# Experts read the raw rows in steps of four columns, and one more expert weight unit is loaded ahead

## What is computed

```python
logits = einsum('bsd,de->bse', h, w_router)      # h = rmsnorm_2(x, norm_moe), 16 experts
aff = softmax(logits)
vals, idx = top_k(aff.T, cap)                    # cap = 32 tokens for each expert
xg = h[bidx, idx]                                # the gathered rows, 32 x 1024 per expert
h1, h3 = xg @ w1, xg @ w3                        # 1024 x 1024 each, per expert
out = (silu(h1) * h3) @ w2                       # 1024 x 1024
x = x + scatter_add(out * vals)
```

## Time and profile before

| | |
|---|---|
| median of three runs | 1896.9 us |
| the profiled execution, its own time | 1900.6 us |
| span from first to last instruction | 1898.8 us |
| PE busy, PE weight loads busy | 1550.6 us, 1135.1 us |
| DVE, ACT, POOL busy | 612.3, 500.4, 193.9 us |
| mean granted TensorE clock | 0.942 |
| moved by DMA | 563.65 MB, mean 297 GB/s |

### The profile page before, as it was taken

The page is one execution under the profiler, slowest core; times in us unless marked ns, Lnnn a source line. Parts: engine busy times, 40 slices in busy tenths (PEclk is TensorE's granted clock), DMA queues, the critical chain, the costliest instruction groups (busy, mean ns, idle before and its releaser), DMA issues.

```text
span 1898.8 us, 29516 instructions
## 1 busy us (share of the span) xinstructions
PE 1550.6 (82%) x12506; PEld 1135.1 (60%) x12506; DVE 612.3 (32%) x923; ACT 500.4 (26%) x910; POOL 193.9 (10%) x214
## 2 busy tenths in 40 slices
PE   7999999999999999665655656999998666666656
PEld 6999899998898886232322323997883322323225
DVE  3456534577556353000000002655450000000005
ACT  3433333556444432000000002454330000000003
POOL 0043000011041100000000002410100000000003
PEclk9999999999999999898888888999999888989888
DMA  8564549432554569999999999545399999999994
GB/s 284 164 219 168 195 155 301 152 111 91 178 172 136 177 233 386 425 427 424 427 426 424 427 426 377 180 152 178 128 378 394 426 425 424 427 425 427 426 425 152
DMA packets 166894, 563.65 MB, mean 297 GB/s; under 512 B 10559, under 2 KB 120027, under 8 KB 133896
## 3 DMA queue, kind: packets, MB, share of 16 engines
q1 hardware_dynamic: 159012, 552.08, 75.1%
q10 hardware_dynamic: 7780, 10.10, 1.6%
HBM read 561.08 MB, written 5.23 MB: 298 GB/s over the span
## 4 chain that ended last, share of the span: by engine, by line
PE 52%; DMA 36%; DVE 4%; ACT 3%; issue 3%; POOL 1%; SPq 0%; ACTq 0%; DVEq 0%; POOLq 0%
DMA ring<-in_moe_w 36%; PE bank L965 21%; PE bank L1213 7%; PE bank L1622 5%; PE bank L921 4%; PE bank L1060 3%; PE bank L1645 2%; PE bank L1276 2%; ACT ring_r L1695 1%; ACT big L1743 1%; PE bank L1090 1%; PE bank L1480 1%; PE bank L1285 1%; PE bank L1037 1%; PE bank L1651 1%
## 5 line engine op out<-in xcount | busy, mean ns | idle before, releaser
L1622 PE MATMUL bank<-ring,big 128*32 128x256 f32 x3840 | 281.3, 443 | 195.7 <-DMA ring<-in_moe_w 193.2
L1622 PEld LDWEIGHTS bank<-ring,big 128*32 128x32 f32 x3840 | 147.0, 123 | 335.8 <-issue 295.4
L965 PE MATMUL bank<-big_r,ring_r 128*128 128x256 f32 (+1 forms) x2760 | 344.1, 285 | 0.0
L965 PEld LDWEIGHTS bank<-big_r,ring_r 128*128 128x128 f32 (+1 forms) x2760 | 335.1, 191 | 3.0 <-issue 2.2
L2092 DVE TENSOR_TENSOR ring_r<-ring,ring_r 128x2048 fp32r<-128x2048 f32 (+2 forms) x105 | 243.0, 2319 | 135.3 <-ACT ring_r L1695 133.9
L1743 ACT ACTIVATE big<-bank 128x512 f32<-128x512 f32 (+2 forms) x186 | 87.9, 491 | 571.6 <-PE bank L921 366.8
L1695 ACT ACTIVATE ring_r<-ring 128x2048 fp32r<-128x2048 f32 (+2 forms) x109 | 204.2, 1881 | 10.4 <-DMA ring<-in_ev_w_out 5.1
L1645 PE MATMUL bank<-ring,big 128*32 128x512 f32 x1024 | 136.7, 634 | 74.0 <-DMA ring<-in_moe_w 55.5
L2479 DVE SCALAR_TENSOR_TENSOR big<-big,bank 128x256 f32<-128x256 f32 x32 | 13.5, 421 | 463.9 <-ACT big L1995 463.9
L1213 PE MATMUL bank<-ring_r,big_r 128*128 128x512 f32 x576 | 135.7, 395 | 0.7 <-DVE big_r L2099 0.7
L921 PE MATMUL bank<-big 128*128 128x128 f32 (+6 forms) x636 | 105.1, 292 | 35.7 <-ACT big L1743 18.2
(11 more groups left out here) (204 smaller groups left out, 1512.8 us busy)
## 6 DMA issues: line engine op xcount, KB each, us to landing
ring<-in_moe_w SPq DMA_DIRECT2D x120, 2048.0 KB, 23.7
ring<-in_moe_w SPq DMA_DIRECT2D x128, 1024.0 KB, 24.9
ring<-in_w_in SPq DMA_DIRECT2D x28, 1024.0 KB, 5.4
ring<-in_od_w_in SPq DMA_DIRECT2D x22, 1024.0 KB, 6.5
ring<-in_ev_w_in SPq DMA_DIRECT2D x20, 1024.0 KB, 7.3
big<-in_moe_w SPq DMA_DIRECT2D x8, 2048.0 KB, 11.2
ring<-in_ev_w_out SPq DMA_DIRECT2D x8, 1024.0 KB, 5.0
ring<-in_od_cmp_w SPq DMA_DIRECT2D x8, 1024.0 KB, 8.1
```

What stands on the lines that cost most here:

```text
L965: ins = unit[0].mark(mm(dst, lhsT, rhs, start=start and n == 0, stop=stop and n == len(terms) - 1))
L1622: ins = mm(banks[5 + up][32 * j:32 * j + 32, 0:256], xg[:, k, q, :], wv[:, r, 256 * j:256 * (j + 1)], start=k == 0, stop=k == KC - 1)
```

## The change

- The gather reads x itself as PE's stationary operand. The old copy put columns r, r+4, r+8, ... side by side; now the operand is a view of x with a step of four columns (16 bytes). `rows_u` and the `u_ready` wait are gone.
- The root goes into the one-hot matrix: DVE writes `onehot` in two halves of 128 columns, and after each half multiplies it by `rstd` into the new `rows_hot`, which is the gather's moving operand. `onehot` itself is kept for POOL. `rows_hot` lies where the `pw` product's input was, so DVE first waits for the last `pw` product.
- The gather's 16 products run by half of the columns, then by half of the rows, then four column blocks.
- `tile_ss` writes its unread squares to `pwb`, so `u` is free from the end of the attention. Into it SP loads expert 1's first down unit (`row_spare`, 1 MB), right after spares 1 and 2. Expert 1's other three down units go into the ring, and its fourth slot is passed over: PE marks it itself after the expert's down products.

```diff
-        spare_at = [G_at + 8 * T + 4 * D * i for i in range(SPARES - 1)] + [uT_at]
+        rows_hot = view(G_at + 8 * T + 4 * D * (SPARES - 1), P, TT, BATCH * CAP)
+        spare_at = [G_at + 8 * T + 4 * D * i for i in range(SPARES - 1)] + [uT_at, u_at]
...
+                def row_spare(row):
+                    src = flat(a["moe_w2_2"])[row:row + 2 * P, :].rearrange("(p r) c -> p (r c)", r=2)
+                    sp.dma_start(view(u_at, P, 2 * D), src).then_inc(spare_in[ROW_SPARE], 16)
+
-                def down(row):
-                    for i in range(4):
+                def down(row, first=0):
+                    for i in range(first, 4):
                         deep(a["moe_w2_2"], row + 256 * i, 2)
...
                 spare(1)
                 spare(2)
+                row_spare(first + D)
                 deep(ups[0], first, 4)
...
                 deep(ups[1], first + D, 4)
-                down(first + D)
+                down(first + D, 1)
+                w.next()
...
                 def batch(b):
                     g4 = l * (NE // BATCH) + b
-                    pe.wait_ge(onehot_ready, g4 + 1)
-                    for t in range(TT):
-                        pe.wait_ge(u_ready[t], rows_at(l, 1) + 1)
-                    for k in range(KC):
+                    for half in range(2):
                         for t in range(TT):
-                            ins = mm(banks[4 + 2 * (k // 4)][:, (k % 4) * P:(k % 4 + 1) * P], u[:, t, k * P:(k + 1) * P],
-                                     onehot[:, t].rearrange("p q s -> p (q s)"), start=t == 0, stop=t == TT - 1)
-                        if k % 4 == 3:
-                            ins.then_inc(gathered, 1)
+                            pe.wait_ge(onehot_ready, TT * g4 + t + 1)
+                            rows = x[:, t, 512 * half:512 * (half + 1)].rearrange("p (q r) -> p r q", r=4)
+                            for k in range(4):
+                                ins = mm(banks[4 + 2 * half][:, k * P:(k + 1) * P], rows[:, k, :], rows_hot[:, t, :],
+                                         start=t == 0 and k == 0, stop=t == TT - 1, skip_group_check=True)
+                        ins.then_inc(gathered, 1)
...
-                            U = Unit()
+                            U = Spare(l, ROW_SPARE) if isinstance(b, int) and (q, j) == (1, 0) else Unit()
...
+                        if isinstance(b, int) and q == 1:
+                            pe.sem_inc(units_in[w.next()[0]], 16)
+                            Unit.before += 1
...
-                tile_ss(0, x[:, 0, :])
+                tile_ss(0, x[:, 0, :], rest=pwb)
                 tile_raw(l, 0, gl[:, 8:])
-                rows_u(0)
...
+                wait_done(dve, l, "pw", 3)
                 stand(dve)
...
-                    V.tensor_tensor(onehot, con("iota").unsqueeze(1).unsqueeze(1).broadcast_to([P, TT, BATCH, CAP]),
-                                    idxT[:, :, bass.ds(b * BATCH, BATCH)].unsqueeze(3)
-                                    .broadcast_to([P, TT, BATCH, CAP]), ALU.is_equal).then_inc(onehot_ready, 1)
+                    for t in range(TT):
+                        steps.link(V.tensor_tensor(onehot[:, t], con("iota").unsqueeze(1).broadcast_to([P, BATCH, CAP]),
+                                                   idxT[:, t, bass.ds(b * BATCH, BATCH)].unsqueeze(2)
+                                                   .broadcast_to([P, BATCH, CAP]), ALU.is_equal))
+                        V.tensor_scalar(rows_hot[:, t, :], onehot[:, t].rearrange("p q s -> p (q s)"), rstd[:, t:t + 1], None,
+                                        ALU.mult).then_inc(onehot_ready, 1)
```

More of the change, by code:

```diff
@@ L290 @@
 SPARES = 4
+ROW_SPARE = SPARES
 PLE_AT, PER_LAYER = slots_of(PLE_UNITS, _n + NE * MOE_UNITS - 2 * SPARES)
@@ L567, in build @@
         uTh_ready = sem("uT_high")
-        spare_in = [sem(f"spare_in{i}") for i in range(SPARES)]
+        spare_in = [sem(f"spare_in{i}") for i in range(SPARES + 1)]
         units_in = [sem(f"unit_in{s}") for s in range(RING)]
@@ L688, in rows_at @@
         def rows_at(l, j):
-            return j if l is None else 3 + j + 2 * l
+            assert l is None or j == 0
+            return j if l is None else 3 + l
         def out_at(l, j):
@@ L910, in __init__ @@
                     pe.wait_ge(spare_in[i], 16 * (l + 1))
-                    s.words, s.first, s.step = view(spare_at[i], P, 4, D), True, Unit.before
+                    s.words = view(spare_at[i], P, 2 if i == ROW_SPARE else 4, D)
+                    s.first, s.step = True, Unit.before
                     Unit.before = 0
@@ L1678, in _, with tile_ss @@
             act.dma_start(perow, a["od_cmp_pe"][0].rearrange("v l d -> (v l) d")).then_inc(rows_in, 16)
-            def tile_ss(t, src, sums=ss):
-                A(u[:, t, :], src, ACT.Square, accum_out=sums[:, t:t + 1]).then_inc(norm_ss[t], 1)
+            def tile_ss(t, src, sums=ss, rest=u):
+                A(rest[:, t, :], src, ACT.Square, accum_out=sums[:, t:t + 1]).then_inc(norm_ss[t], 1)
             def tile_scale(l, j, t, src):
@@ L1969, in _ @@
                              banks[5 + h % 2][0:MLN + MLR, :].rearrange("p (h c) -> p h c", h=2), QT_ready)
[L1970 to L1974, removed]
                 act.wait_ge(x_ready, 4 * out_at(l, 2) + 2)
-                tile_ss(0, x[:, 0, :])
+                tile_ss(0, x[:, 0, :], rest=pwb)
                 tile_raw(l, 0, gl[:, 8:])
-                rows_u(0)
                 tile_raw(l, 1, gl[:, 8:])
                 act.wait_ge(x_ready, 4 * out_at(l, 2) + 4)
-                tile_ss(1, x[:, 1, :])
+                tile_ss(1, x[:, 1, :], rest=pwb)
                 for t in range(TT):
@@ L1986, in _ @@
                       scale=rstd[:, t:t + 1], accum_out=rt[:, 2 + t:3 + t]).then_inc(rt_exp, 1)
-                evacuate(l, "pw", 0)
-                rows_u(1)
-                for i in range(1, 4):
+                for i in range(4):
                     evacuate(l, "pw", i)
@@ L2464, in _ @@
                     g4 = l * (NE // BATCH) + b
-                    steps.enter(b, BATCH)
-                    V.tensor_tensor(onehot, con("iota").unsqueeze(1).unsqueeze(1).broadcast_to([P, TT, BATCH, CAP]),
-                                    idxT[:, :, bass.ds(b * BATCH, BATCH)].unsqueeze(3)
-                                    .broadcast_to([P, TT, BATCH, CAP]), ALU.is_equal).then_inc(onehot_ready, 1)
+                    steps.enter(b, BATCH + TT)
+                    for t in range(TT):
[4 more added lines that the diff above has]
+                                        ALU.mult).then_inc(onehot_ready, 1)
                     for n in range(2):
@@ L2657, in _ @@
                         if q == 0:
-                            pool.wait_ge(onehot_ready, l * (NE // BATCH) + b + 1)
+                            pool.wait_ge(onehot_ready, TT * (l * (NE // BATCH) + b + 1))
                         else:
```

## The result

The changed kernel takes 1904.09 us (median of six runs, 1902.15 to 1907.12); the kernel before took 1896.95 us in six runs beside it. The ratio is 1.0041, 95% interval 1.003 to 1.0052: **7.1 us slower** (about 6 to 10 by the interval), where 1.6 us faster was forecast. It lies above the forecast's range too, and is the size of the third rival's upper end and a little more.

The account below looks back on a forecast made before the run. Expert weight traffic at 426 GB/s was taken to bound the expert stages. The extra unit's -2.17 us plus 2 x 0.3 us for the gather gave -1.57 us, from 1896.9 to 1895.3 us; range 1892.4 to 1902.6.

Parts of the forecast that it names:

- the third rival: First gather of each layer: the stepped read is slow, 2.6 to 3.9 us per layer, total 1901.7 us; chance 0.28.
- The stepped read: PE's weight loads in each layer's first gather, reading x every 16 bytes: forecast to cost nothing extra.
- The one from DVE's rows: Gather weight load priced from DVE's stepped write: 0.70 ns more per element, 200 ns per load.
- The two reasons for zero: For a free stepped read in the gather: both priced rows are writes, and PE takes an element only every 0.85 ns.
- The extra unit: 1 MB of expert 1 preloaded in each layer: wins 0.96 us in the first, 1.21 us in the second.
- the third idle place: DMA gap of about 2 us from 749 us, before expert 2's stream, until PE frees slots for its load.
- the fourth, shallow place: Not forecast: DMA flow dips after expert 2's first piece, 356 for 430 GB/s 18 us after the first up product.
- The empty slot has no further price that I see: Passed-over ring slot: expert 1's later slots come free 0.9 us later, unnoticed by DMA with 8 MB of expert 2 issued.
- The forecast's sum for the second layer: Bytes counted to find expert 2's effective stream start, 1440.26 us, 2.81 us behind its issue, leaving 1.21 us to win.
- The way to the first gather: DVE's halved one-hot and scaling before PE's first gather: +0.3 us per layer, bounds 0.1 and 0.75.
- Nothing for ACT's copies: Dropping ACT's `rows_u` copies, 2.1 us per half, four times in all, gains nothing because PE's work covers them.
- Batches 1 to 3: Later gathers and DVE's extra operations are hidden before later-arriving weights; without that cover, under 1 us a batch.

## Why the prediction was wrong

1. **The stepped read: the step that failed.** The prediction put "I take zero for the forecast", with 2.6 to 3.9 us per layer as a rival's price. Measured: 7.73 - 3.84 = 3.89 us, the very upper end, 7.8 us for both layers. The estimate from ACT's stepped write (1.03 ns more per element, 242 ns per load) hit the 242 ns: the load itself grew by 137 ns, from 192 to 329, where 132 was estimated. The one from DVE's rows fell short, and those two rows are different operations, so their difference is not the write's alone. The two reasons for zero did not hold: reads pay as writes do, and PE's slower pace leaves no cover, since the load takes 110 ns of a 120 ns interval. The nearest rows all said 200 ns or more, and the forecast set them aside without a row of its own. The Trainium skill (SBUF — State Buffer, "Door 1: The DMA port swizzle") states the rule that decided: full bandwidth wants two accesses per 16-byte line. The runs agree: two accesses per line (step 2) cost 121 ns for 115, one per line 237 to 243 ns. The same passage also gives four fp32 words as the distance that is free; the runs do not bear that out, for a step of three costs 178 ns and a step of four 237.

2. **The extra unit.** That it would not count whole, because the load behind the third idle place hangs on PE's release of a slot, was right: the gap is there, ended by an issue at 754.05, 9.45 us behind the one at 744.60, as before. SP's two issues:

```profile
744.60 0.80 SPq L788 DMA_DIRECT2D ring<-in_moe_w  x2
...
754.05 0.33 SPq L788 DMA_DIRECT2D ring<-in_moe_w  x1
```

The size was off: about 0.4 us per layer for 1.1. The term left out is the fourth, shallow place (0.3 MB, 0.7 us). "The empty slot has no further price that I see" was wrong as well: moving it back let in 1.6 us of bytes in one layer, of which the release of the first load explains 0.9. The forecast's sum for the second layer has a slip that moves nothing: 170 + 4,190 + 566 - 4,194 is 732 KB, not 742, which is 0.02 us.

3. **The way to the first gather.** +0.3 us was forecast. From the start of the one-hot to the gather it is 0.67 us (733.89 to 734.56) for 0.48, so +0.2. The second one-hot overlaps the first scaling, and the second half is ready at 735.03, before the gather's first quarter ends. Right.

4. **Nothing for ACT's copies.** Right. The eviction that stood behind `rows_u` comes at the same distance from its product, 1.93 us after that product's start, as before:

```profile
725.69 1.89 PE L975 MATMUL bank<-ring,big 128*128 128x256 f32 x8
...
727.62 0.60 ACT L1793 ACTIVATE big<-bank 128x512 f32<-128x512 f32 x1 [1.98 <-PE bank L975]
```

5. **Batches 1 to 3.** Their gathers took 7.7 us each as well, and PE is busy 265 of 400 us for 250, while DMA keeps 425 GB/s. Cover held, at a much larger price than I had it cover.

By these sizes the sum is 2 x (3.9 + 0.2 - 0.4) = +7.4 us; measured were 7.1, and the unit's term alone is uncertain by some tenths of a us per layer. In the traces, from the first spare's issue to the last scatter product, the two expert stages last 491.6 and 490.8 us before, and 494.9 and 495.3 after: 7.8 us more.

## What to carry to other kernels

When a copy that only reorders data is dropped, the reader pays for the order. Price the access step by 16-byte lines, and ask which of the reads stands where nothing covers it: here two of eight gathers made the whole loss. Memory gained for a preload is worth only what the next gate behind it lets through. Find who opens that gate before counting bytes, and count the ring slots that the bookkeeping leaves empty.

## What the runs showed of the hardware

- TensorE's operand reads from SBUF cost about 1.85 ns per 16-byte line entered, per fp32 instruction: from start to start 115 ns per 128-column instruction at a step of 1 word, 121 at 2, 178 at 3, 237 at 4, 243 at 8, and 231 at 4 on the moving operand.
- In a weight stream that saturates DMA the length of the contiguous pieces shows, or the order that goes with it: 426 GB/s with pieces of 16 KB for two thirds of the bytes and 8 KB for the rest, 421 with 8 KB throughout, 413 with 4 KB for the two thirds.
